# The last merged slice and the last weight unit before the output projection, exchanged

## The reference, cut to what matters

```
ys = jnp.stack([y_a, y_b, y_c, y_d], axis=2)
gates = jax.nn.sigmoid(h @ w_gate + b_gate).reshape(bsz, s, N_BRANCH, D_MODEL)
merged = jnp.einsum('bsnc,ncd,bsnd->bsd', ys, w_branch, gates)
return merged @ w_o
```

## Time and profile before

| | us |
|---|---|
| median of 3 runs | 839.17 (838.19 to 842.02) |
| the profiled execution, its time | 838.19 |
| its span, first to last instruction | 836.5 |
| TensorE busy | 787.1 (94%) |
| VectorE busy | 660.3 (79%) |
| ScalarE busy | 511.9 (61%) |
| GpSimd busy | 21.7 (3%) |
| mean granted TensorE clock | 0.981 of full speed |

### The profile page before, as it was taken

One profiled execution on the slowest core, in us unless ns is written; L12 is line 12 of the kernel. 1 busy time (PEld: TensorE's weight loads), 2 busy tenths in 40 slices (PEclk: granted clock), 3 DMA queues, 4 the chain that ended last, 5 costly groups with the idle time before them and its releaser, 6 DMA issues.

```text
span 836.5 us, 13286 instructions
## 1 busy us (share of the span) xinstructions
PE 787.1 (94%) x4822; PEld 696.8 (83%) x4822; DVE 660.3 (79%) x854; ACT 511.9 (61%) x567; POOL 21.7 (3%) x32
## 2 busy tenths in 40 slices
PE   6999999999769999999899999999967999999996
PEld 6899999998558877877789999999846878787874
DVE  5857996498577889998674899559666989989887
ACT  6526555662547778787543555664364787868874
POOL 4110000000000000000001000000000000000000
PEclk9999999999989999999999999999998999999999
DMA  8867254366315999999646644337431899999994
GB/s 244 295 203 250 95 168 142 101 227 214 112 53 198 339 342 341 356 335 330 224 131 201 204 148 153 126 101 277 152 101 51 280 326 360 339 353 342 357 336 167
DMA packets 80309, 189.80 MB, mean 227 GB/s; under 512 B 12022, under 2 KB 23944, under 8 KB 80264
## 3 DMA queue, kind: packets, MB, share of 16 engines
q1 hardware_dynamic: 80264, 189.20, 65.4%
HBM read 188.12 MB, written 1.05 MB: 226 GB/s over the span
## 4 chain that ended last, share of the span: by engine, by line
PE 62%; issue 24%; DVE 6%; ACT 5%; DMA 2%; POOL 1%; ACTq 0%; SPq 0%; DVEq 0%; POOLq 0%
PE bank L1244 18%; PE bank L1246 18%; PE bank L1245 18%; ACT w_hi L482 3%; DVE w_lo L743 2%; PE bank L1533 2%; PE bank L1562 2%; PE bank L1587 1%; DMA raw<-in_w_e_up 1%; DMA raw<-in_w_in 1%; DVE xn L1013 1%; PE bank L1506 1%; ACT xn L493 1%; ACT a_hi L661 0%; DVE xn L1019 0%
## 5 line engine op out<-in xcount | busy, mean ns | idle before, releaser
L743 DVE TENSOR_TENSOR w_lo<-raw,w_hi 128x2048 fp32r<-128x2048 f32 (+1 forms) x183 | 402.9, 2216 | 98.5 <-ACT w_hi L482 97.0
L482 ACT ACTIVATE w_hi<-raw 128x2048 fp32r<-128x2048 f32 (+1 forms) x183 | 338.8, 1857 | 187.2 <-PE bank L1246 143.2
L1244 PE MATMUL bank<-a_hi,w_hi 128*128 128x256 f32 x704 | 201.9, 287 | 2.8 <-DVE a_lo L818 2.8
L1245 PE MATMUL bank<-a_hi,w_lo 128*128 128x256 f32 x704 | 200.5, 285 | 0.0
L1246 PE MATMUL bank<-a_lo,w_hi 128*128 128x256 f32 x704 | 200.5, 285 | 0.0
L1244 PE MATMUL bank<-w_hi,y_lo 128*128 128x512 f32 x432 | 171.3, 397 | 0.8 <-DVE y_lo L1186 0.8
L1246 PE MATMUL bank<-w_lo,y_lo 128*128 128x512 f32 x432 | 168.8, 391 | 0.0
L1244 PEld LDWEIGHTS bank<-a_hi,w_hi 128*128 128x128 f32 x704 | 136.4, 194 | 4.4 <-DVE w_lo L743 3.0
L1245 PEld LDWEIGHTS bank<-a_hi,w_lo 128*128 128x128 f32 x704 | 136.4, 194 | 0.1
L1246 PEld LDWEIGHTS bank<-a_lo,w_hi 128*128 128x128 f32 x704 | 136.3, 194 | 0.0
L1245 PE MATMUL bank<-w_hi,y_hi 128*128 128x512 f32 x288 | 112.3, 390 | 0.0
(11 more groups left out here) (288 smaller groups left out, 865.7 us busy)
## 6 DMA issues: line engine op xcount, KB each, us to landing
raw<-in_w_e_gate SPq DMA_DIRECT2D x72, 512.0 KB, 4.4
raw<-in_w_e_up SPq DMA_DIRECT2D x72, 512.0 KB, 5.8
raw<-in_w_e_down SPq DMA_DIRECT2D x72, 512.0 KB, 5.0
raw<-in_w_gate SPq DMA_DIRECT2D x56, 512.0 KB, 4.6
raw<-in_w_in SPq DMA_DIRECT2D x38, 512.0 KB, 6.4
raw<-in_w_branch SPq DMA_DIRECT2D x16, 512.0 KB, 4.1
raw<-in_w_o SPq DMA_DIRECT2D x16, 512.0 KB, 4.1
raw<-in_w_gate SPq DMA_DIRECT2D x16, 256.0 KB, 2.8
```

Of the source, the lines that this page charges most:

```text
L482: a.activation(w_hi[:, at.slot(n, PART), 0:w], raw[:, slot, 0:w], ACT.Copy).then_inc(hi_done, 1)
L743: v.tensor_tensor(w_lo[:, part, 0:w], raw[:, slot, 0:w], w_hi[:, part, 0:w].bitcast(F32), ALU.subtract).then_inc(split_done, 1)
L1244: mm(ps, a2[0], b2[0], start=first, stop=False, skip_group_check=shared)
L1245: mm(ps, a2[1], b2[0], start=False, stop=False, skip_group_check=shared)
```

## The change

Two lines move, in both layers. On ScalarE `merged_hi(7)` goes ahead of `hi(at, 35)`. On VectorE `merged_low(7)` goes ahead of `lo(at, 35)`. No instruction is added or taken away, and no semaphore, count or operand differs. TensorE, GpSimd and SP have the same streams as before.

```diff
@@ -638,8 +638,8 @@
                 merged_hi(5)
                 hi(at, 34)
                 merged_hi(6)
+                merged_hi(7)
                 hi(at, 35)
-                merged_hi(7)
                 at = At(l, before, True)
                 hi(at, 0)
                 hi(at, 1)
@@ -1038,8 +1038,8 @@
                 merge(6)
                 lo(at, 34)
                 merge(7)
+                merged_low(7)
                 lo(at, 35)
-                merged_low(7)
                 at_m = At(l, before, True)
                 lo(at_m, 0)
                 for i in range(4):
```

## The result

| | before | after |
|---|---|---|
| median of 6 runs each, us | 838.82 (835.81 to 842.02) | 846.32 (844.29 to 849.99) |
| ratio | 1 | 1.0097, 95% interval 1.0066 to 1.0127 |
| span of the profiled execution, us | 836.5 | 848.4 |
| mean granted TensorE clock | 0.981 | 0.971 |

The kernel became slower by 0.97%, 8.1 us (5.5 to 10.6), where 4.86 us (0.58%) was forecast.

A forecast was written before the change was run, and what follows sets the result against it. The prediction took TensorE, busy 787.1 of 836.5 us, as the bound, waiting on `lo(35)` at the place of the change. It added 2 x 2.43 = 4.86 us to 839.17, giving 844.0 us, with 841.2 to 846.4 for 8 in 10.

The forecast's parts named there:

- Slice 7 isn't late, unit 35 is: In the projection, TensorE's slice 6 waits for `lo(35)`, while slice 7 has 1.19 us to spare.
- `hi(35)` behind `merged_hi(7)`, 2.43 us a layer: On ScalarE `hi(35)` loses its idle-time cover, so VectorE's `lo(35)` starts 2.43 us later in each layer.
- Rival A: Only VectorE's order counts, as ScalarE does `hi(35)` in its idle time: +1.9 us, 841.1; chance 0.05.
- B: Slack in the expert loop, if paced by supply, takes the delay in: 839.2 us; chance 0.05.
- E: Faster, if TensorE waited at slice 7: saves 0.51 us in the first layer, less in the second: 838.3; chance 0.03.
- The delay passes through: Nothing behind slice 6, in router stage or expert loop, absorbs the late start: 2 x 2.43 = 4.86 us.
- rival D: The shift puts the low clock stretch at 237 to 244 on idle time, winning 2.1 us a layer at most: 839.8; chance 0.04.
- rival C: TensorE's clock falls in the 2.9 us gap before slice 6: 845.5 us in one layer, 847.0 in both; chance 0.10.

The follow-up runs named there:

- after_pe_order: The changed kernel with TensorE doing slices 0 to 3 for the second 128 tokens ahead of slices 6 and 7 for the first: 839.89 us, ratio 0.9991.
- pad_long: The kernel before with 18 constant matmuls on TensorE ahead of slice 6, a delay of 3.4 us a layer: 847.08 us, ratio 1.0078.
- after_fill12: The changed kernel with 12 constant matmuls in TensorE's gap before slice 6: 845.00 us, ratio 1.0075.
- after_again: The changed kernel measured once more, with no edit: 846.9 us, ratio 1.0095 against the kernel before.
- before_look_a: The kernel before, without edit, profiled again to see where its low clock stretches lie; no median time is given.
- before_look_b: The kernel before, without edit, profiled once more for the same question; no median time is given.
- vector_only: The kernel before with only VectorE's two lines exchanged, ScalarE's order kept: 843.98 us, ratio 1.0051.
- vector_look: vector_only profiled a second time, without further edit; no median time is given.

## Why the prediction was right and wrong

- **Slice 7 isn't late, unit 35 is.** Right: wherever TensorE idles ahead of slice 6, its matmul is released by L743.
- **`hi(35)` behind `merged_hi(7)`, 2.43 us a layer.** Right to 0.01 us in both layers, and shown by parts: 0.96 us with VectorE's exchange alone, 2.4 with ScalarE's alone. ScalarE didn't overtake: `hi(35)` stood behind `merged_hi(7)` while the engine idled 4.09 us. That agrees with the Trainium skill, page "TensorE: Matmul & The Clock Gate", section "Architectural detail: the array is 16× 32×32, not 1× 128×128", by which ScalarE takes its queue strictly first in, first out.
- **Rival A** falls with the rows, **B** and **E** with the time; after_pe_order shows that TensorE's wait was the way by which the exchange reached the end.
- **The delay passes through.** Right, but not alone. The step that failed is the end of this sum, "2 x 2.43 = 4.86 us" with the clock's share taken as nothing, and the sentence under rival D, "Nothing says that it falls better rather than worse, and the same play is in every run". Its term measured about 3 us: 8.1 against 4.86. D named the right stage, but the shift made the low stretches there longer and not cheaper.
- **What stands in its place, first part: rival C.** I gave it 0.10 and reasoned that 2.9 us of idle time is nearer to 2.38, behind which the clock stayed, than to 5.14. The clock fell in four of six places, for 3.4 or 6.8 us, and cost 1.4 to 2.9 us each. The neighbour at 2.38 us was one sample. The same place, ahead of L1562 (L1565 with added lines), has 2.2 to 2.4 us of idle time in all fourteen profiles, and in two of them, pad_long and after_fill12, the clock stood at half behind it; after_again shows that the gap of 2.8 gives both outcomes too. That C's price for both layers, 847.0, comes near the measured time is in part luck: in after_again the clock fell behind neither gap, and the kernel was 8.0 us slower all the same. pad_long, timeline and stretch of TensorE:

```profile
404.07 0.50 PE L1565 MATMUL bank<-a_hi 128*128 128x512 f32 x1 [2.40 <-DVE a_lo L1216]
```

```profile
404.70:408.00 3.30, 3.30 (x11) 0.50 0.95 322
```

- **Second part: the router stage.** The kernel before isn't a neutral mark. Its first layer has 10 us at the lower level in three profiles of three, and a shift by 1 us, by order or by constant work, made it 17 us or more in three of three. Its second layer isn't as steady: 10, 17 and 21 us in the three profiles. The pure delays cost 5.1 us in all for 1 us a layer and 6.5 for 3.4 us a layer. That this is a matter of where the low stretches fall against the work fits both; it isn't shown, nor is what fixes their places, and the second layers of before_look_a, before_look_b and pad_long didn't follow. What is shown by the times of all executions is that the extra goes with more time at the lower level. How the 3 us divide between the two parts stays open: after_fill12, at +6.3, can't be told from +4.9 or +8.1.

## What to carry to other kernels

Before two instructions change places in a queue, ask for each engine what it would have done in the idle time ahead of the one that waits: an early unit of weights made in such time is free, and behind the wait it is on the path in full. A consumer in fixed order can be given other work that is ready, and the same late unit then costs nothing. Where TensorE has a stage with gaps, price a shift of it too, and measure a pure delay beside the change before blaming the change for the difference.

## What was not expected of the hardware

- The cost of a delay needn't be its length: +5.1 us (3.3 to 7.0) for 2.1 us, +6.5 (4.4 to 8.7) for 6.9.
- An idle time of 2.6 to 2.8 us between dense matmuls lowered the granted clock to 0.50 in four of six places; one of 2.2 to 2.4 us in two of fourteen; one of 1.2 to 1.3 us in none of four (vector_only and vector_look). The Trainium skill, page "TensorE: Matmul & The Clock Gate", section "Part 1: The HAM clock gate", puts the cost of the ramp from half rate to full rate under 1% of a typical kernel span. The trace agrees: a fall behind the gap cost 1.4 to 2.9 us of some 840, 0.2 to 0.35%. But the change itself was forecast at 0.58%, so what is small against the span isn't small against the change.
- A float32 matmul of 128 columns of a constant is recorded as two and takes 0.22 us, as long as one of 512 columns in the kernel's own format (0.23).
